# Product with `w_out` as seven half-size products, the `ple` product inside it, the gate product started tile by tile

## The chip, the core and the metric

The kernel runs on one core of one Trainium2 chip. The metric is the time of one execution in device microseconds (us); the median of three runs counts. The core has five instruction queues that run side by side and meet only through semaphores: PE (TensorE, matrix products and transposes), DVE (VectorE), ACT (ScalarE), POOL (GpSimd) and SP, which here only issues transfers.

## What is computed

A first block with attention and a short convolution, then a second block of two layers. Everything is float32, with 512 tokens of width 1024. The change lies at the end of the first block:

```python
mixed = jnp.concatenate([attn, conv_out], axis=-1) @ w_out[i]     # 512x1024 @ 1024x1024
x = x + rms_norm(mixed, post_norm_gain[i])                        # called x1 below

e = rms_norm(p[i] @ w_ple_proj[i], ple_norm_gain[i])              # 512x256 @ 256x1024
x = x + jax.nn.sigmoid(x @ w_ple_gate[i]) * e                     # 512x1024 @ 1024x1024
```

`attn` and `conv_out` are 512 columns wide each. Behind this comes the second block, whose first product (`v4`, with a 1024x2048 part of `a_w_in_2`) is already computed by seven half-size products for each half of its columns.

## The kernel before

**Split operands.** Each float32 operand of a large product is kept as a rounded part `hi` and a rest `lo`, and each product is three matmuls: hi·hi, hi·lo, lo·hi (`exact`, the lines 2076 to 2078). So each weight and each activation must be split before PE can use it. For the weights, a transfer of 512 KB brings half a unit into a room of `raw` or `gain`, one engine writes `whi` and one writes `wlo`. Units "by two" are split by ACT (`whi`, 1024 wide) and DVE (`wlo`, 1024 wide); all others by POOL alone (`whi` line 841, `wlo` line 850, 512 wide each). `whi` and `wlo` hold two units; a unit takes the slot of the unit two before it.

**Order.** `tensor_order` writes out by hand in what order PE works through its blocks, and `bank_of` says in which of eight PSUM banks a block's result lands. The other queues are written out by hand as well. Every queue is worked in order, so an instruction that waits holds up all that stand behind it on its engine.

**Around the change.** The last jobs of the projection stage are four heads of attention and the four feature tiles of the convolution. Their results go to `actB_hi`/`actB_lo`: attention in tiles 0 to 3 (DVE line 1609), convolution in tiles 4 to 7 (ACT line 1026, DVE line 1548). Then PE runs, in this order:

- `wo`: four units (two halves of the columns, two halves of the rows of `w_out`), each over four token tiles of 128: 192 matmuls of 512 columns. The results stay in the eight banks. In between, `p` is transposed.
- `ple`: 48 matmuls. Between its tiles, the pairs of transposes of x1 (line 2173).
- `gate`, first half of the columns: unit 0 (rows 0 to 511) over four token tiles, the transposes of the group weights (`wt`, line 2312), then unit 1, and so on.

x1 comes about like this: ACT squares the banks of `wo` with a sum (`square`, line 950); POOL makes the root (`root`, lines 795 and 798); DVE multiplies the bank by the root and the gain and adds the result to `resid` (`post`, lines 1618 and 1622, the wait being `x1_ready`); PE transposes `resid`; ACT writes `actA_hi` (`turned`, line 961) and DVE `actA_lo` (`rest`, line 1421, semaphore `lo_x1`). A gate block of token tile t waits for `lo_x1` of that tile.

**Seven products, as `v4` has them.** The activations are cut in two by tokens and in two by features, the weights in two by rows and columns. The seven products use sums of quarters. The four sums of activations are made one after the other: DVE `act_sum` (line 1679) writes a sum, ACT `sum_hi` (line 1122) its `hi`, DVE `act_sum_lo` (line 1683) its `lo`. The sums of weights are made by transfers that add to what lies in the room (`add_load`, issued by POOL). A product is 24 matmuls into two banks; `keep_v4` (line 1126) or `combine` (line 1696) takes it out, and `combine` adds it to parts of the result in `big`.

## Time and profile before

| | |
|---|---|
| median of three runs | 885.27 us (885.25 to 885.89) |
| the profiled execution | 885.75 us, span 884.0 us |
| PE busy | 868.2 us, 98% of the span |
| DVE, ACT, POOL busy | 537.2, 360.3, 542.8 us |
| granted TensorE clock | full in all 40 slices |
| bytes moved | 102.65 MB, mean 116 GB/s |

The span runs from the first to the last instruction; 1.75 us of the execution lie around it. "Busy" adds up the time in which an engine had work running. PE's rows overlap: a matmul of 512 columns is shown with 0.39 us, while the next starts 0.23 us after it. So the distance from one start to the next is the price of a matmul, and a wait shows as a larger distance between two starts.

### The profile page before, as it was taken

The page shows a single profiled execution, that of the slowest core. Times are in us where ns is not written, and L with a number is a line of the kernel's source. Part 1 is how long each engine was busy: PE and PEld are TensorE (multiplying, and loading weights), DVE is VectorE, ACT ScalarE, POOL GpSimd, SP SyncE. Part 2 cuts the span into 40 slices and gives each one's busy share as a digit, 9 for nine tenths or more (in the row PEclk, how much of TensorE's full clock was granted, in tenths as well). Part 3 has the DMA queues.
Part 4 walks back from the last instruction along what each step waited for, and adds up shares of the span by engine and source line. Part 5 has one row for each costly group of instructions (what it writes and reads, how often), then busy time and mean ns, then how long its engine had stood idle before and what let it go on. Part 6 is the DMA issues. An engine that isn't in the chain of part 4 may idle for free.

```text
span 884.0 us, 11936 instructions
## 1 busy us (share of the span) xinstructions
PE 868.2 (98%) x4220; PEld 722.0 (82%) x4220; DVE 537.2 (61%) x880; ACT 360.3 (41%) x804; POOL 542.8 (61%) x604
## 2 busy tenths in 40 slices
PE   8999999999999999999999999999997999999997
PEld 6888888888888787888888888888887888888886
DVE  6125648875035489775765535556996457788624
ACT  4123333431134377546112321113775536767622
POOL 7766556587789832317975038771359798566352
PEclk9999999999999999999999999999999999999999
DMA  7533231342322468885742253526962222112202
GB/s 198 167 120 96 74 92 51 96 143 92 128 90 96 124 146 177 208 203 190 162 124 95 73 190 96 125 90 152 217 180 71 72 73 93 51 49 72 73 1 95
DMA packets 81517, 102.65 MB, mean 116 GB/s; under 512 B 11826, under 2 KB 54322, under 8 KB 81459
## 3 DMA queue, kind: packets, MB, share of 16 engines
q1 hardware_dynamic: 72752, 85.12, 30.1%
q0 software_dynamic: 8704, 16.78, 11.2%
q8 instruction: 34, 0.56, 0.3%
q14 instruction: 25, 0.20, 0.1%
q10 hardware_dynamic: 2, 0.00, 0.0%
HBM read 99.79 MB, written 2.10 MB: 115 GB/s over the span
## 4 chain that ended last, share of the span: by engine, by line
PE 88%; POOL 4%; DVE 2%; DMA 2%; ACT 2%; issue 1%; POOLq 0%; DVEq 0%; ACTq 0%
PE bank L2076 26%; PE bank L2078 26%; PE bank L2077 26%; PE bank L2319 2%; PE bank L2347 1%; PE bank L2173 1%; DMA gain<-in_a_w_in 1%; DVE wlo L1667 1%; POOL wlo L850 1%; PE bank L2292 1%; PE bank L2342 1%; PE bank L2341 1%; DMA raw<-in_a_w_in 1%; POOL ms L795 1%; POOL whi L841 1%
## 5 line engine op out<-in xcount | busy, mean ns | idle before, releaser
L850 POOL TENSOR_TENSOR wlo<-raw,whi 128x512 fp32r<-128x512 f32 x204 | 280.4, 1404 | 0.7 <-ACT whi L972 0.7
L841 POOL TENSOR_SCALAR whi<-raw 128x512 fp32r<-128x512 f32 x202 | 140.8, 733 | 188.1 <-PE bank L2078 179.1
L2076 PE MATMUL bank<-actB_hi,whi 128*128 128x512 f32 (+1 forms) x416 | 159.6, 384 | 0.6 <-POOL wlo L850 0.6
L2077 PE MATMUL bank<-actB_lo,whi 128*128 128x512 f32 (+1 forms) x416 | 158.7, 381 | 0.0
L2078 PE MATMUL bank<-actB_hi,wlo 128*128 128x512 f32 (+1 forms) x416 | 158.5, 381 | 0.0
L2076 PE MATMUL bank<-whi,actA_hi 128*128 128x512 f32 x318 | 125.9, 396 | 1.2 <-DVE actA_lo L1421 0.7
L2078 PE MATMUL bank<-whi,actA_lo 128*128 128x512 f32 x318 | 124.0, 390 | 0.0
L2077 PE MATMUL bank<-wlo,actA_hi 128*128 128x512 f32 x318 | 123.9, 390 | 0.0
L2076 PEld LDWEIGHTS bank<-actB_hi,whi 128*128 128x128 f32 x416 | 78.3, 188 | 15.4 <-issue 1.1
L2078 PEld LDWEIGHTS bank<-actB_hi,wlo 128*128 128x128 f32 x416 | 78.2, 188 | 15.2
L2077 PEld LDWEIGHTS bank<-actB_lo,whi 128*128 128x128 f32 x416 | 78.3, 188 | 14.1
L2076 PE MATMUL bank<-actA_hi,whi 128*128 128x512 f32 x224 | 87.9, 392 | 0.0
L2077 PE MATMUL bank<-actA_lo,whi 128*128 128x512 f32 x224 | 87.4, 390 | 0.0
L2078 PE MATMUL bank<-actA_hi,wlo 128*128 128x512 f32 x224 | 87.3, 390 | 0.0
L2076 PEld LDWEIGHTS bank<-whi,actA_hi 128*128 128x128 f32 x318 | 59.7, 188 | 15.3 <-issue 1.9
L2078 PEld LDWEIGHTS bank<-whi,actA_lo 128*128 128x128 f32 x318 | 59.7, 188 | 12.6
L2077 PEld LDWEIGHTS bank<-wlo,actA_hi 128*128 128x128 f32 x318 | 59.8, 188 | 12.0 <-issue 0.2
L2076 PE MATMUL bank<-whi,actB_hi 128*128 128x512 f32 x144 | 56.5, 393 | 0.2 <-DVE wlo L1667 0.2
L2078 PE MATMUL bank<-whi,actB_lo 128*128 128x512 f32 x144 | 56.1, 390 | 0.0
L2077 PE MATMUL bank<-wlo,actB_hi 128*128 128x512 f32 x144 | 56.0, 389 | 0.0
L1776 DVE TENSOR_TENSOR acc<-acc,gcv 128x512 f32<-128x512 f32 x16 | 15.6, 974 | 58.3 <-ACT gcv L1228 58.3
L2078 PEld LDWEIGHTS bank<-actA_hi,wlo 128*128 128x128 f32 x224 | 42.1, 188 | 8.9
(269 smaller groups left out, 1579.4 us busy)
## 6 DMA issues: line engine op xcount, KB each, us to landing
raw<-in_a_w_in SPq DMA_DIRECT2D x44, 512.0 KB, 4.2
raw<-in_w_in SPq DMA_DIRECT2D x32, 512.0 KB, 3.9
raw<-in_b_w_in SPq DMA_DIRECT2D x16, 512.0 KB, 3.4
raw<-in_a_w_out SPq DMA_DIRECT2D x12, 512.0 KB, 3.3
gain<-in_a_w_out POOLq DMA_DIRECT2D x9, 512.0 KB, 8.2
raw<-in_w_out SPq DMA_DIRECT2D x8, 512.0 KB, 3.4
raw<-in_w_ple_gate SPq DMA_DIRECT2D x8, 512.0 KB, 3.3
gain<-in_a_w_in POOLq DMA_DIRECT2D x8, 512.0 KB, 7.7
```

The lines of the kernel that those rows point to most:

```text
L795: pool.tensor_scalar(m, ss[:, n, t, 0:1], ss[:, n, t, 1:2], EPS, ALU.add, ALU.add).then_inc(ms_ready, 1)
L841: pool.tensor_scalar(H, src[:, i * HALF:(i + 1) * HALF], 1.0, 1.0, ALU.mult, ALU.mult).then_inc(w_hi, 1)
L850: ins = pool.tensor_tensor(L, src[:, i * HALF:(i + 1) * HALF], H.bitcast(f32), ALU.subtract)
L1667: V.tensor_tensor(L, src, H.bitcast(f32), ALU.subtract).then_inc(w7_lo, 1)
L1776: V.tensor_tensor(acc[:, f % 2, :], acc[:, f % 2, :], gcv[:, f % 2, 0:S], ALU.mult).then_inc(zu_made, 1)
L2076: M(out_, whi_, xhi_, start=start, stop=False)
L2077: M(out_, whi_, xlo_, start=False, stop=False)
L2078: return M(out_, wlo_, xhi_, start=False, stop=stop)
L2173: ins = nc.tensor.transpose(bank[:, k * P:(k + 1) * P], src, ident[:, :])
L2292: ins = M(bank[:, qt * P:(qt + 1) * P], wgtT1[:, k * P:(k + 1) * P], tile(vtok, k)[:, h * P:(h + 1) * P], start=k == 0, stop=k == qt)
L2319: ins = M(bank[:, n * P:(n + 1) * P], big[:, n, f * P:(f + 1) * P], wcT[:, (f // 2) * P:(f // 2 + 1) * P], start=True, stop=True)
L2341: M(out_, q, khi(g)[:, keys], start=True, stop=False)
```

## The change

The four `wo` units become seven products `("S", "wo", q, r)`, q from 0 to 6, with two row tiles r. The quarters of `w_out` and their sums lie in rooms A, B and G; three of the sums are made by adding transfers. The result goes to `big` (`out_wo`) by the same `keep` and `combine` as in `v4`, and no longer stays in the banks. ACT and DVE split the weights of products 0, 1, 2, 3, 4 and 6 and of `ple`; POOL splits those of product 5. `ple` stands between products 4 and 5, with nothing in between its tiles. Its raw result goes to other parts of `big` (`e_raw`). The transposes of x1 stand behind product 6, each pair just ahead of the gate tile that reads it. `post` reads `out_wo` from `big` instead of a bank. The attention and convolution results also stay whole in `kT` and `zaT`, from which the sums of activations are made; for this the convolution's last multiplication writes to `zaT`.

```diff
-    u += [("wo", 2 * c + kh, "T", "w_out", 4 * kh, 512 * c) for c in range(2) for kh in range(2)]
+    u += [("wo", q, "S", "w_out", 0, 0) for q in range(5)]
     u += [("ple", 0, "P", "w_ple_proj", 0, 0)]
+    u += [("wo", q, "S", "w_out", 0, 0) for q in (5, 6)]
...
-    o += [("Th", "wo", 0, 0, t) for t in range(T)] + [("tr", "p", 0, k) for k in range(2)]
-    o += [("T", "wo", 0, 0, t) for t in range(T)]
-    o += [("T", "wo", 0, 1, t) for t in range(T)]
-    o += [("T", "wo", 1, kh, t) for kh in range(2) for t in range(T)]
-    for t in range(T):
-        o += [("ple", t, c) for c in range(2)]
-        if t:
-            o += [("tr", "x1", t - 1, j) for j in range(2)]
-    o += [("T", "gate", 0, 0, 0)] + [("tr", "x1", 3, j) for j in range(2)]
-    o += [("T", "gate", 0, 0, t) for t in range(1, T)] + [("wt", j) for j in range(2)]
+    o += [("S", "wo", q, r) for q in range(4) for r in range(2)] + [("tr", "p", 0, k) for k in range(2)]
+    o += [("S", "wo", 4, r) for r in range(2)] + [("ple", t, c) for t in range(T) for c in range(2)]
+    o += [("S", "wo", q, r) for q in (5, 6) for r in range(2)]
+    turn = lambda name, t: [("tr", name, t, j) for j in range(2)]
+    o += turn("x1", 0) + [("Th", "gate", 0, 0, 0)] + turn("x1", 1) + [("T", "gate", 0, 0, 0), ("T", "gate", 0, 0, 1)]
+    o += turn("x1", 2) + [("T", "gate", 0, 0, 2)] + turn("x1", 3) + [("T", "gate", 0, 0, 3)]
+    o += [("wt", j) for j in range(2)]
...
-            after[at("ple", 0, 0)] = [lambda: root("m1", 0, D)]
-            after[at("ple", 0, 1)] = [lambda t=t: root("m1", t, D) for t in range(1, T)]
+            after[at("wo", 5, 1)] = [lambda: root("m1", 0, D)]
+            after[at("gate", 0, 0) - 0.5] = [lambda: root("m1", 1, D)]
+            after[at("gate", 0, 0)] = [lambda: root("m1", 2, D)]
+            after[at("gate", 0, 1) - 0.5] = [lambda: root("m1", 3, D)]
...
+            after[at("b", 1, 1)] = [lambda: add_load("wo", 0, 3)]
+            after[at("zc", 1, 1)] += [lambda n=n: add_load("wo", 0, n) for n in (4, 6, 7)]
...
+            sum_hi(0, "wo")
+            hi_7("wo", 2)
+            for r in range(2):
+                keep_7("wo", 0, r)
+            sum_hi(1, "wo")
+            hi_7("wo", 3)
...
+            for t in range(2):
+                square_m1(2 + t, 1)
+            for t in range(2):
+                square_m1(t, 1)
+            for t in range(2):
+                square_m1(2 + t, 0)
+            for t in range(T):
+                for j in range(2):
+                    turned("x1", t, j)
...
-                    V.scalar_tensor_tensor(acc[:, c, :], psum[t + 4 * c][:, :], rstd[:, NORMS[name], t:t + 1],
+                    V.scalar_tensor_tensor(acc[:, c, :], out_wo(t, c), rstd[:, NORMS[name], t:t + 1],
```

**ACT, from the last convolution tile to `ple`.** Before, ACT copies the transposed `p` (line 959) and then only squares the banks of `wo`:

```order
L959 ACTIVATE actA_hi<-bank 128x512 [waits pe_block] x2
L950 ACTIVATE junk,ss<-bank 128x512 [waits attn_sq,pe_block]
L950 ACTIVATE junk,ss<-bank 128x512 [waits squared_m1,pe_block] x7
L1072 ACTIVATE big<-bank 128x512 [waits pe_block]
L950 ACTIVATE junk,ss<-bank 128x512 [waits squared_m1]
```

Now there stand here the `hi` parts of the sums of activations (line 1057) and of the weights of products 2 to 4 (line 1042), the copies of product 0 (line 1061) and two squares (line 982). The names `t_added` and `t3_added` are semaphores of the adding transfers:

```order
L1057 ACTIVATE actA_hi<-big 128x1024 [waits s7_made]
L1042 ACTIVATE whi<-raw 128x1024 [waits t_added0,pe_block]
L1042 ACTIVATE whi<-raw 128x1024 [waits t_added1]
L1061 ACTIVATE big<-bank 128x512 [waits pe_block] x2
L1057 ACTIVATE actA_hi<-big 128x1024 [waits s7_made]
L1042 ACTIVATE whi<-gain 128x1024 [waits t3_added0,pe_block]
L1042 ACTIVATE whi<-gain 128x1024 [waits t3_added1]
L1057 ACTIVATE actA_hi<-big 128x1024 [waits s7_made]
L982 ACTIVATE junk,ss<-big 128x512 [waits attn_sq,c7_made]
L982 ACTIVATE junk,ss<-big 128x512 [waits squared_m1,c7_made]
L1042 ACTIVATE whi<-raw 128x1024 [waits t_added0,pe_block]
```

Each `hi` of a sum now stands ahead of the two `hi` of the weights of the same product. In `v4` (before and now) both weight copies, or at least the first, stand ahead of the sum.

**DVE, where x1 is made.** Before, the four `post` stand one after the other, with the rests of one tile in between:

```order
L1618 SCALAR_TENSOR_TENSOR acc<-bank,rstd,gain 128x512 [waits rstd_m1,gain_in1]
L1618 SCALAR_TENSOR_TENSOR acc<-bank,rstd,gain 128x512
L1622 TENSOR_TENSOR resid<-resid,acc 128x1024 [waits post_scaled]
...
L1421 TENSOR_TENSOR actA_lo<-bank,actA_hi 128x4x128 [waits hi_x1] x2
```

Now the two combinations of product 6 (line 1686, waits `c7_made,pe_block`) stand between them, and the first operand of a `post` (line 1725) is `big`:

```order
L1725 SCALAR_TENSOR_TENSOR acc<-big,rstd,gain 128x512 [waits rstd_m1,gain_in1]
L1725 SCALAR_TENSOR_TENSOR acc<-big,rstd,gain 128x512
L1729 TENSOR_TENSOR resid<-resid,acc 128x1024 [waits post_scaled]
L1686 TENSOR_TENSOR big<-bank,big 128x512 [waits c7_made,pe_block]
L1725 SCALAR_TENSOR_TENSOR acc<-big,rstd,gain 128x512 [waits x1_ready,rstd_m1]
...
L1686 TENSOR_TENSOR big<-bank,big 128x512 [waits c7_made,pe_block]
L1476 TENSOR_TENSOR actA_lo<-bank,actA_hi 128x4x128 [waits hi_x1] x2
```

**PE, the transposes of x1.** Before, the twelve matmuls of a `ple` tile stand between two pairs of transposes (a pair is eight):

```order
L2173 MATMUL bank<-ident,resid 128x128 [waits x1_ready,squared_e]
L2173 MATMUL bank<-ident,resid 128x128 x3
...
L2076 MATMUL bank<-whi,actA_hi 128x512 [waits w_lo,lo_p,post_scaled]
L2077 MATMUL bank<-wlo,actA_hi 128x512
L2078 MATMUL bank<-whi,actA_lo 128x512
```

Now the matmuls of the gate follow directly on the transposes whose tile they read (`lo_x1`), tile 0 in two halves (`Th`, then `T`) with the transposes of tile 1 between them:

```order
L2268 MATMUL bank<-ident,resid 128x128 [waits x1_ready,c7_made]
L2268 MATMUL bank<-ident,resid 128x128 x3
...
L2171 MATMUL bank<-whi,actA_hi 128x512 [waits w_lo,lo_x1]
L2172 MATMUL bank<-wlo,actA_hi 128x512
L2173 MATMUL bank<-whi,actA_lo 128x512
```

## Rows read from the trace of the kernel before

**Rows 1.** The page's head and busy times (busy us, share of the span, instructions)

```profile
span 884.0 us, 11936 instructions
...
PE 868.2 (98%) x4220; PEld 722.0 (82%) x4220; DVE 537.2 (61%) x880; ACT 360.3 (41%) x804; POOL 542.8 (61%) x604
```

**Rows 2.** The chain of work that ended last, by engine

```profile
PE 88%; POOL 4%; DVE 2%; DMA 2%; ACT 2%; issue 1%; POOLq 0%; DVEq 0%; ACTq 0%
```

**Rows 3.** Busy time by engine: `wo`, then `ple` to the gate's unit 0

```profile
214.63:259.07 44.44, 44.44 (x201) 36.88 (x200) 9.52 (x10) 7.65 (x19) 33.58 (x36) 1.00 0.35 119
259.07:284.48 25.41, 25.41 (x130) 21.29 (x128) 15.53 (x19) 14.10 (x34) 24.64 (x26) 1.00 0.31 103
```

**Rows 4.** PE in order of time (start, us, what): the stage's edges

```profile
214.63 0.39 PE L2076 MATMUL bank<-whi,actB_hi 128*128 128x512 f32 x1
...
222.80 1.03 PE L2173 MATMUL bank<-ident,smC 128*128 128x128 f32 x8
...
259.07 0.39 PE L2076 MATMUL bank<-whi,actA_hi 128*128 128x512 f32 x1
...
284.48 1.04 PE L2312 MATMUL bank<-ident,gcv 128*128 128x128 f32 x8
```

**Rows 5.** DVE in order of time, around `wo` and where x1 is made

```profile
212.44 1.77 DVE L1609 TENSOR_TENSOR actB_lo<-big,actB_hi 128x512 fp32r<-128x512 f32 x1
...
216.19 1.79 DVE L1541 TENSOR_TENSOR acc<-acc,gcv 128x512 f32<-128x512 f32 x1
217.90 2.79 DVE L1548 TENSOR_TENSOR actB_lo<-acc,actB_hi 128x512 fp32r<-128x512 f32 x2
...
253.75 1.41 DVE L1618 SCALAR_TENSOR_TENSOR acc<-bank,rstd,gain 128x512 f32<-128x512 f32 x2 [28.40 <-POOL rstd L798]
255.19 1.61 DVE L1622 TENSOR_TENSOR resid<-resid,acc 128x1024 f32<-128x1024 f32 x1
...
276.66 1.29 DVE L1421 TENSOR_TENSOR actA_lo<-bank,actA_hi 128x512 fp32r<-128x512 f32 x2 [1.70 <-ACT actA_hi L961]
```

**Rows 6.** DVE in order of time inside `v4`

```profile
348.13 1.22 DVE L1679 TENSOR_TENSOR big<-big 128x1024 f32<-128x1024 f32 x1
349.26 1.22 DVE L1667 TENSOR_TENSOR wlo<-raw,whi 128x1024 fp32r<-128x1024 f32 x1
...
352.75 3.67 DVE L1696 TENSOR_TENSOR big<-bank,big 128x512 f32<-128x512 f32 x6
```

**Rows 7.** ACT in order of time: a square, a pair of x1, `v4` weights

```profile
261.13 0.59 ACT L950 ACTIVATE junk<-bank 128x512 f32<-128x512 f32 x1
261.60 0.20 ACT L950 ACTIVATION_READ_ACCUMULATOR junk<-bank 128x1 f32 x1
...
276.03 1.08 ACT L961 ACTIVATE actA_hi<-bank 128x512 fp32r<-128x512 f32 x2 [1.90 <-PE bank L2173]
...
347.17 1.99 ACT L1118 ACTIVATE whi<-raw 128x1024 fp32r<-128x1024 f32 x2
```

**Rows 8.** POOL in order of time: one root, one half unit of weights

```profile
258.05 0.30 POOL L795 TENSOR_SCALAR ms<-ss 128x1 f32<-128x1 f32 x1
258.44 0.58 POOL L798 TENSOR_TENSOR rstd<-ms,mhalf 128x1 f32<-128x1 f32 x1
...
272.58 1.20 POOL L841 TENSOR_SCALAR whi<-raw 128x512 fp32r<-128x512 f32 x2
273.76 2.53 POOL L850 TENSOR_TENSOR wlo<-raw,whi 128x512 fp32r<-128x512 f32 x2
```

**Rows 9.** Two DVE groups of one form, each over the whole program

```profile
L1903 DVE SCALAR_TENSOR_TENSOR resid<-big,rstd,resid 128x512 f32<-128x512 f32 x8 | 8.7, 1131 | 1.6 <-POOL rstd L798 1.6
...
L2065 DVE SCALAR_TENSOR_TENSOR resid<-big,rstd,resid 128x512 f32<-128x512 f32 x8 | 5.7, 749 | 1.4 <-POOL rstd L798 1.4
```

**Rows 10.** Transfers by line, KB each, median us to landing

```profile
raw<-in_a_w_in POOLq DMA_DIRECT2D x8, 512.0 KB, 7.6
```

**Rows 11.** PE in order of time, transposes near the program's start

```profile
7.94 1.92 PE L2173 MATMUL bank<-ident,tok 128*128 128x128 f32 x8
```

More of the change, by code:

```diff
@@ L66 @@
 WHOLE = {n: k for k, n in enumerate(n for n, u in enumerate(UNITS) if u[2] != "S")}
-BY_TWO = [n for n, u in enumerate(UNITS) if u[2] == "S" or u[:2] in (("z4", 0), ("z4", 4))]
+BY_TWO = [n for n, u in enumerate(UNITS) if u[2] == "S" and u[:2] != ("wo", 5)
+          or u[:2] in (("ple", 0), ("z4", 0), ("z4", 4))]
 TWO_NO = {n: k for k, n in enumerate(BY_TWO)}
@@ L105, in room_of @@
         return ROOM_A[j]
-    if s == "k5":
+    if s in ("k5", "ple"):
         return "K"
@@ L180 @@
 BANKS_F = ((1, 2, 0, 4), (5, 3, 6, 7))
-HEADS = {("v", 0, 0, t): 2 for t in range(T)} | {("wo", 0, 0, t): 3 for t in range(T)}
-HEADS |= {("gate", 1, 1, 3): 2}
+HEADS = {("v", 0, 0, t): 2 for t in range(T)}
+HEADS |= {("gate", 0, 0, 0): 2, ("gate", 1, 1, 3): 2}
 def tensor_order():
@@ new lines, in act_sum @@
+            def act_sum(i, s="v4"):
+                upper, lower = slice(0, S // 2), slice(S // 2, S)
+                one, two = feature(s, 0), feature(s, 1)
+                a11, a12, a21, a22 = one[:, :, upper], two[:, :, upper], one[:, :, lower], two[:, :, lower]
+                if i:
+                    dve.wait_ge(s7_lo, SUMS7[s] + i)
+                elif s == "v4":
+                    dve.wait_ge(h_copied, 2 * T)
+                else:
+                    dve.wait_ge(lo["attn"], NH1)
+                    dve.wait_ge(lo["conv"], 4)
+                place, first, second, op = ((a22, a21, a22, ALU.subtract), (a21, a11, a21, ALU.subtract),
+                                            (a22, a22, a11, ALU.subtract), (a22, a12, a22, ALU.add))[i]
+                V.tensor_tensor(place, first, second, op).then_inc(s7_made, 1)
@@ new lines, in act_sum_lo, with combine @@
+            def act_sum_lo(i, s="v4"):
+                dve.wait_ge(s7_hi, SUMS7[s] + i + 1)
+                V.tensor_tensor(s7(actA_lo, i), feature(s, 1 - (i == 1))[:, :, S // 2:S], s7(actA_hi, i).bitcast(f32),
+                                ALU.subtract).then_inc(s7_lo, 1)
+            def combine(g, m, place, other, op, waits, s="v4", rows=range(2)):
+                for r in rows:
+                    t, c = place
+                    u, d = other
+                    b = ("S", s, 7 * g + m, r)
+                    dve.wait_ge(pe_block, BLOCK[b])
+                    if waits:
+                        dve.wait_ge(c7_made, 14 * GROUP7[s, g] + waits + r)
+                    else:
+                        dve.wait_ge(x7_kept, 2 * GROUP7[s, g] + r + 1)
+                    V.tensor_tensor(out7(s, g, t + r, c), psum[bank_of(b)][:, :], out7(s, g, u + r, d), op)\
+                        .then_inc(c7_made, 1)
```

316 lines of the change are left out of this document (178 added, 138 removed).

## The prediction

> **What bounds the kernel now.** First the page's head and busy times [rows 1]: PE has work in 868.2 of 884.0 us, the next engine in 542.8. The chain that ended last says the same: 88% of it is PE [rows 2]. The table by stretches then narrows it down to the changed place [rows 3]: `wo` takes 44.44 us, `ple` with gate unit 0 25.41 us, and PE is busy in all of both. So two things count: how many matmuls go, and how long PE waits for operands that it does not wait for now. DVE is busy for 9.52 and 15.53 us there, ACT for 7.65 and 14.10. They have room on average; the question is whether they are in time.
>
> The price of a matmul follows from the two stretches. The first holds 192 matmuls and one group of eight transposes, the second 96 matmuls and four such groups. That gives 0.227 us for a matmul and 0.9 for a group. So a product of 24 costs 5.44 us, a gate tile of 12 costs 2.72, the half tile at its head 1.36. Nothing else in these stretches fits between: the edges lie at 214.63, 259.07 and 284.48 [rows 4].
>
> **What goes.** 192 matmuls become 168: 24 x 0.227 = 5.4 us less. That is all the change can give, 0.6% of the time.
>
> **Durations for what comes in.** DVE: a 1024-wide operation starts 1.13 us after the one before it, six combinations take 3.67, so 0.6 each [rows 6]. A free `post` is 1.2 for its two products and 1.15 for its sum, 2.4 together. ACT: two 1024-wide copies take 1.99 less the overlap, 0.95 each; a square with its sum 0.7 to 0.8; a pair of copies of x1 1.08, with DVE's first rest done 1.2 after the transposes [rows 5, 7]. POOL: a root 1.0, the `hi` of a half unit 1.2, its `lo` 2.5 [rows 8].
>
> **Front, products 0 to 4 and `ple`.** The clock of before is used. Product 0 needs the last attention rest, done at 212.44 + 1.77 = 214.2 [rows 5], and starts at 214.6 as now. It ends at 220.1. Product 1 needs the convolution's last rest. DVE now puts the two weight rests of product 1 (2.3 us) ahead of it. The slow 1.79 and 2.79 us [rows 5] become short again, as POOL no longer splits weights here: 216.2 + 0.6 + 0.6 + 2.3 + 0.6 = 220.4. Wait 0.3. Then begins the loop over the sums of activations: sum (DVE 1.13), its `hi` (ACT 0.95), first half of the weights' `hi` (ACT 0.95), weight rest, rest of the sum, second weight rest (DVE 3 x 1.13), 0.2 for hand-overs, together 6.6. A product lasts 5.44. In `v4` this loop is closed by DVE alone, 4 x 1.13 = 4.6, as ACT has a weight copy ready early [rows 6]; here ACT makes the sum's `hi` first and DVE stands idle for two copies. Product 2 is just met (+0.2), product 3 comes 1.2 late (232.5 for 231.3), product 4 is 0.8 late behind the transposes of `p`, because two squares (1.5) stand ahead of its weights. `ple` follows the same two queues: sum 3, its `hi` and rest, two copies and two rests of its own weights, `p` copied and split last. This is done at 247.5, while product 4 ends at 245.1: 2.5 late. Front: 0.3 + 0.2 + 1.2 + 0.8 + 2.5 = **5.0 us**. Products 5 and 6 have `ple` (10.9 us) as cover for their weights. If ACT had the weights early, the front would wait 1 us at least (the convolution and `p`).
>
> **Tail, x1 and the gate.** Set 0 at the end of product 6. Before, `ple` covered this chain. Now only product 6 (5.44) covers tile 0, and nothing covers the rest. Tile 0 is ready at about 0: the squares of product 5 end at -4.7, root -3.7, `post` 2.4 to 3.7. Its transposes end at 0.9. But ACT's copies of tile 0 stand behind the squares of product 6, and the last of those waits for a combination that stands behind `post` of tile 1 on DVE.
>
> - All free: 0.6 (combination) + 2.4 (`post` 1) + 0.6 (combination) + 0.8 (square) + 0.6 (copy) + 0.6 (rest) = 5.6, so PE waits 4.7. The second half of gate unit 0 is split behind roots 2 and 3: 1.2 more. Tile 1 is in time. Tiles 2 and 3 each wait for their own copy and rest, 1.2 each. Sum 8.3.
> - With POOL in the way: `post` now reads `big` and `gain`, both in SBUF, while POOL splits gate weights beside it. Before it read a bank, and took 1.41 for two with POOL busy; its SBUF-only sum took 1.61 for 1.15 [rows 5]. The attention rest took 1.77 and the convolution product 1.79 where 0.68 is free. So each of the three operations may lose up to a whole POOL operation (1.05 to 1.25), and `post` becomes 5.2 on the mean. Then tile 0: 0.6 + 5.2 + 0.6 + 0.8 + 0.6 + 0.6 = 8.4, wait 7.5. POOL, delayed the same way, has the second half of unit 0 at 12.0, for 10.7: 1.3. DVE then makes rests to 9.0, `post` 2 to 14.2, rest of tile 1 at 14.9, for 13.4: 1.5. `post` 3 ends at 20.7, rest of tile 2 at 21.4, for 18.5: 2.9. Tile 3 waits 1.2 for copy and rest. Sum **14.4**.
>
> I take the second, because the rows with POOL's split directly beside show nearly a full operation lost. The mean of a whole group says less: one form takes 1131 ns where POOL is at work and 749 where it is not [rows 9], 0.4 for an operation; with that `post` is 3.6 and the tail about 11, which lies between the bounds.
>
> The Trainium skill ("SBUF — State Buffer", section "SBUF: two separate sides") says that a VectorE instruction with two SBUF inputs and a GpSimd instruction share a port pair as an exclusive lock, held for the whole instruction. By that rule every operation of `post` may wait for a whole `lo` of POOL (1.27), and the sum would be +15; by the mean of the group it would be +11.
>
> Later stages: PE stays the bound, and nothing there waits long enough to give the time back.
>
> **Sum.** -5.4 + 5.0 + 14.4 = +14.0. The profiled execution has 884.0 in the span and 1.75 around it; the change gives 898.0 + 1.75 = 899.8. The median lies 0.5 below that execution, so **899.3 us**. The ends: front 1 and tail 8.3 give +3.9, front 5 and tail 8.3 +7.9, front 5.5 and tail 16 +16.
>
> **Rivals.**
> - *The port costs little.* Speaks for it: POOL also has roots and waits in between, and the group mean in rows 9. Then front 5.0, tail 8.3: 893.2.
> - *The clock falls in the long wait.* PE stands still for 7.5 us. Near the start eight transposes took 1.92 us [rows 11] where later 1.03 is usual [rows 4], half speed. Tile 0 at half speed costs 2.7 + 0.9 more, of which the waits for weights and tile 1 take up 1.3 + 1.5 again: 900 to 903. Against it: nothing in before stands still so long, so no row tests it.
> - *An adding transfer is late.* They land 7.6 us after issue [rows 10]. The one for product 2 is issued at about 208 and needed at 222; those for product 4 at about 227 and 237; each has some 2 to 6 us to spare. Late by as much again, 904.
> - *Faster.* ACT and DVE run ahead as in `v4` (front 0), and tile 0 is all that waits, 4.7: -5.4 + 4.7 = 884.6. This decides as soon as all waits together fall below 5.4. Against it: in the front the order of ACT's queue alone gives 1.2 a product, and in the tail `post` 1 stands ahead of the last square in any case.
>
> In a sentence apart: the Trainium skill ("TensorE: Matmul & The Clock Gate", section "Part 1: The HAM clock gate") says that an idle TensorE is put back to 1.2 GHz; by that rule the second rival holds, and the time is up to 903.
>
> **Chances.** Forecast (waits 17 to 22, 896 to 902) 0.57; port cheap (891 to 896) 0.16; clock 0.13; late transfer 0.05; faster 0.05; no change 0.04. The likeliest gives 899.3. The range must leave out 0.2: 892 to 904 leaves out the last two and the far parts of the second and the fourth. What lies within 0.2% (1.8 us) of before can hardly be told from no change. Faster by more 0.05, within 0.04, slower 0.91.
>
> **What the trace after would show.** Each product has 24 matmuls at 0.227. PE has a gap of about 1 us ahead of product 3 and product 4, 2 to 3 ahead of `ple`, none ahead of 5 and 6. Behind the transposes of tile 0 there is the largest gap, 7 to 8 us (5 if the port is free), released by DVE's rest. `post` operations take 1.3 to 1.9 instead of 0.7. The gate's four tiles have gaps before each, falling to 1.2 at tile 3. `wo` to the group transposes takes 69.9 - 5.4 + 19.4 = 83.9 us. Wrong would be: ACT's copies of tile 0 directly behind their transposes, a `post` of 2.4 throughout, or a granted clock below full.

## The result and the profile after

| | before | after |
|---|---|---|
| median | 885.58 us (885.25 to 887.77, 4 runs) | 901.13 us (898.81 to 901.77, 4 runs) |
| profiled execution, its span | 885.75, 884.0 us | 900.76, 898.6 us |

The ratio is 1.0165 with a 95% interval of 1.0141 to 1.019: slower by 15 us. (The median of before is 0.3 above that of the first table, since a fourth run has come in.) Each experiment below is compared with a median of before taken on the same chip; these lie between 885.3 and 886.5.

The page's head, busy times and granted clock in 40 slices, after; [rows 1] shows head and busy times before, where the clock was full in all 40 slices:

```profile
span 898.6 us, 11933 instructions
PE 868.5 (97%) x4196; PEld 719.7 (80%) x4196; DVE 572.0 (64%) x916; ACT 378.8 (42%) x824; POOL 522.5 (58%) x580
PEclk9999999999998999999999999999999999999999
```

PE is busy as long as before with 24 matmuls fewer, and one slice has a clock below full. So something went slower, and something waited. The table by stretches, to be held beside [rows 3]; the stretches are products 0 to 4; `ple` with products 5 and 6; and from the transposes of tile 0 to the group transposes. Columns: stretch and its length, busy time (count) of PE, PE's weight loads, DVE, ACT, POOL, then granted clock, DMA share, GB/s:

```profile
214.30:247.72 33.42, 29.39 (x129) 22.99 (x128) 25.99 (x27) 18.63 (x25) 6.95 (x7) 1.00 0.73 176
247.72:271.21 23.49, 23.49 (x97) 19.18 (x98) 11.94 (x16) 14.07 (x34) 10.37 (x12) 0.93 0.28 92
271.21:298.60 27.39, 17.28 (x81) 13.82 (x80) 22.31 (x21) 5.78 (x12) 26.30 (x28) 0.88 0.24 77
```

There are three kinds of stretch. The first loses time to waits at full clock. The second has PE busy throughout, and loses to the clock alone (0.93 of full on the mean). The third has PE busy for 17.3 of 27.4 us, while DVE and POOL are busy for nearly all of it.

PE's timeline gives every edge (start, duration, line; in brackets the idle time and who ended it), as [rows 4] does for before:

```profile
214.33 0.39 PE L2171 MATMUL bank<-whi,actB_hi 128*128 128x512 f32 x1
220.16 0.47 PE L2171 MATMUL bank<-whi,actB_hi 128*128 128x512 f32 x1 [0.22 <-issue]
232.63 0.47 PE L2171 MATMUL bank<-whi,actA_hi 128*128 128x512 f32 x1 [0.99 <-DVE actA_lo L1672]
239.68 0.47 PE L2171 MATMUL bank<-whi,actA_hi 128*128 128x512 f32 x1 [0.44 <-DVE wlo L1644]
247.72 0.47 PE L2171 MATMUL bank<-whi,actA_hi 128*128 128x512 f32 x1 [2.32 <-DVE actA_lo L1473]
271.21 1.03 PE L2268 MATMUL bank<-ident,resid 128*128 128x128 f32 x8
278.70 0.77 PE L2171 MATMUL bank<-whi,actA_hi 128*128 128x512 f32 x1 [6.46 <-DVE actA_lo L1476]
281.39 1.70 PE L2268 MATMUL bank<-ident,resid 128*128 128x128 f32 x8
284.88 0.47 PE L2171 MATMUL bank<-whi,actA_hi 128*128 128x512 f32 x1 [0.40 <-DVE actA_lo L1476]
287.73 1.04 PE L2268 MATMUL bank<-ident,resid 128*128 128x128 f32 x8
290.99 0.47 PE L2171 MATMUL bank<-whi,actA_hi 128*128 128x512 f32 x1 [2.23 <-DVE actA_lo L1476]
293.83 1.03 PE L2268 MATMUL bank<-ident,resid 128*128 128x128 f32 x8
295.88 0.47 PE L2171 MATMUL bank<-whi,actA_hi 128*128 128x512 f32 x1 [1.02 <-DVE actA_lo L1476]
298.71 1.03 PE L2408 MATMUL bank<-ident,gcv 128*128 128x128 f32 x8
```

From these rows the loss is worked out. The whole takes 84.4 us; before it took 69.9. Each piece between two rows holds a known number of matmuls (0.227) and transpose groups (0.9); what is left over is loss. Products 0 to 4 lose 0.4 + 1.6 + 0.7 + 2.6 = **5.3**. From 247.72 to 271.21 stand 96 matmuls (21.8), in 23.5: **1.7**. Behind the transposes of tile 0 comes a wait of **6.6**. The half tile behind it, six matmuls, takes 2.7 where 1.4 is due, and the next transposes 1.46 for 0.9: **1.9** together. Then 0.7 ahead of tile 1, 2.4 ahead of tile 2, 1.2 ahead of tile 3 and 0.2 in between: **4.5**. The sum is 20.0, less 5.4 for the 24 matmuls: +14.5. The spans differ by 14.6, and 0.4 more lies around the span (2.16 for 1.75).

What stands behind the two pieces lost in "busy" time is shown by the granted clock:

```profile
244.00:250.00 6.00, 3.68 (x14) 2.70 (x13) 6.00 (x10) 1.79 (x4) 4.42 (x5) 0.88 0.70 126
250.00:256.00 6.00, 6.00 (x23) 4.80 (x23) 2.40 (x5) 4.41 (x11) 3.64 (x4) 0.83 0.44 149
276.00:280.00 4.00, 1.30 (x3) 1.14 (x4) 2.73 (x5) 1.69 (x4) 3.82 (x7) 0.50 0.26 100
280.00:284.00 4.00, 4.00 (x17) 3.33 (x17) 3.97 (x3) 1.20 (x2) 4.00 (x3) 0.66 0.31 96
```

Both times PE had just stood still, for 2.3 and 6.5 us. Behind the longer wait its matmuls start 0.43 us apart at once, the lower level of 1.2 GHz. Behind the shorter one the first matmuls still start 0.23 to 0.32 apart, and the lower level holds from 248.8 to 251.8.

The tail on DVE, to be held beside [rows 5]: `post`'s two products (L1725) and its sum (L1729), and the rests that PE waits for (L1476):

```profile
271.40 3.37 DVE L1725 SCALAR_TENSOR_TENSOR acc<-big,rstd,gain 128x512 f32<-128x512 f32 x2
274.81 1.23 DVE L1729 TENSOR_TENSOR resid<-resid,acc 128x1024 f32<-128x1024 f32 x1
...
277.90 1.29 DVE L1476 TENSOR_TENSOR actA_lo<-bank,actA_hi 128x512 fp32r<-128x512 f32 x2 [1.27 <-ACT actA_hi L993]
279.11 3.03 DVE L1725 SCALAR_TENSOR_TENSOR acc<-big,rstd,gain 128x512 f32<-128x512 f32 x2
282.17 2.00 DVE L1729 TENSOR_TENSOR resid<-resid,acc 128x1024 f32<-128x1024 f32 x1
285.30 3.44 DVE L1725 SCALAR_TENSOR_TENSOR acc<-big,rstd,gain 128x512 f32<-128x512 f32 x2
288.77 1.52 DVE L1729 TENSOR_TENSOR resid<-resid,acc 128x1024 f32<-128x1024 f32 x1
```

And on ACT, the last square of product 6 and, only behind it, the copies of tile 0, whose transposes had been ready since 272.1:

```profile
276.67 0.63 ACT L982 ACTIVATE junk<-big 128x512 f32<-128x512 f32 x1 [4.42 <-DVE big L1686]
...
277.30 1.06 ACT L993 ACTIVATE actA_hi<-bank 128x512 fp32r<-128x512 f32 x2
```

`post` 1 to 3 take 4.5 to 5.0 us each, from the first product to DVE's next operation; `post` 0, beside less work of POOL, takes 3.2.

### The profile page after: what moved, and what is told of

The parts are those of the page before. It is cut to its first block, busy times and chain, and to the rows that moved or that the text cites. A ratio compares the mean times of both kernels' runs of the same rounds, so it can differ in the third digit from the quotient of the medians.

```text
span 898.6 us, 11933 instructions
## 1 busy us (share of the span) xinstructions
PE 868.5 (97%) x4196; PEld 719.7 (80%) x4196; DVE 572.0 (64%) x916; ACT 378.8 (42%) x824; POOL 522.5 (58%) x580
## 4 chain that ended last, share of the span: by engine, by line
PE 82%; DVE 7%; POOL 4%; ACT 3%; issue 2%; DMA 1%; DVEq 0%; POOLq 0%; SPq 0%; ACTq 0%
PE bank L2171 25%; PE bank L2173 24%; PE bank L2172 24%; DVE wlo L1644 2%; PE bank L2415 2%; POOL wlo L878 1%; PE bank L2443 1%; DVE acc L1725 1%; PE bank L2388 1%; PE bank L2438 1%; DMA raw<-in_a_w_in 1%; PE bank L2437 1%; DVE big L1668 1%; PE bank L2268 1%; POOL rstd L822 1%
## 5 line engine op out<-in xcount | busy, mean ns | idle before, releaser
L878 POOL TENSOR_TENSOR wlo<-raw,whi 128x512 fp32r<-128x512 f32 x188 | 256.6, 1395 | 0.8 <-ACT whi L1004 0.8
L869 POOL TENSOR_SCALAR whi<-raw 128x512 fp32r<-128x512 f32 x186 | 133.8, 757 | 179.4 <-PE bank L2173 173.9
L2171 PE MATMUL bank<-whi,actA_hi 128*128 128x512 f32 x350 | 139.8, 400 | 15.8 <-DVE actA_lo L1476 10.8
L2173 PE MATMUL bank<-whi,actA_lo 128*128 128x512 f32 x350 | 137.5, 393 | 0.0
L2172 PE MATMUL bank<-wlo,actA_hi 128*128 128x512 f32 x350 | 137.5, 393 | 0.0
L2173 PEld LDWEIGHTS bank<-whi,actA_lo 128*128 128x128 f32 x350 | 66.4, 190 | 14.3
L2172 PEld LDWEIGHTS bank<-wlo,actA_hi 128*128 128x128 f32 x350 | 66.4, 190 | 13.4 <-issue 0.2
L1644 DVE TENSOR_TENSOR wlo<-raw,whi 128x1024 fp32r<-128x1024 f32 x28 | 33.4, 1221 | 29.2 <-ACT whi L1042 29.2
L2172 PEld LDWEIGHTS bank<-actA_lo,whi 128*128 128x128 f32 x224 | 42.1, 188 | 8.3
L2171 PEld LDWEIGHTS bank<-actA_hi,whi 128*128 128x128 f32 x224 | 42.1, 188 | 8.3
```

Source lines behind the costliest of these rows:

```text
L869: pool.tensor_scalar(H, src[:, i * HALF:(i + 1) * HALF], 1.0, 1.0, ALU.mult, ALU.mult).then_inc(w_hi, 1)
L878: ins = pool.tensor_tensor(L, src[:, i * HALF:(i + 1) * HALF], H.bitcast(f32), ALU.subtract)
L1644: V.tensor_tensor(L, src, H.bitcast(f32), ALU.subtract).then_inc(w7_lo, 1)
L2171: M(out_, whi_, xhi_, start=start, stop=False)
L2172: M(out_, whi_, xlo_, start=False, stop=False)
L2173: return M(out_, wlo_, xhi_, start=False, stop=stop)
```

## The experiments

All are edits of the changed kernel; from the one with `ple` last on, they build on one another. Times after a label are medians.

### The order of ACT's queue in the front

```diff
-            sum_hi(0, "wo")
             hi_7("wo", 2)
+            sum_hi(0, "wo")
...
-            sum_hi(1, "wo")
             hi_7("wo", 3)
+            sum_hi(1, "wo")
...
             for k in range(2):
                 turned("p", 0, k)
+            sum_hi(3, "wo")
```

`hi_7("wo", 4)` goes ahead of the sum in the same way; on DVE the rest of sum 3 goes behind those of `ple`'s weights and of `p`.

> Only the order of ACT's and DVE's queues in the front changes: both halves of a product's weights are copied before the copy of the sum, and `p` before the last sum. Theory (ACT's order makes the front late): the waits of 1.15 us before product 3 and 2.5 us before `ple` go, and with the second of them the half-speed stretch behind it (1.75 us lost), so 901.1 - 1.1 - 2.4 - 1.7 = 896 us (895 to 897.5), PE gaps in the front below 0.5 us each. Rival (DVE is the late one, the order on ACT is not): the gaps stay and so does the time, 900 to 902. Rival (the clock is not tied to the wait): 897.5 to 898.5, gap gone but the half-speed matmuls remain.

Measured: 895.75 us (895.15 to 896.24), ratio 1.0114 (1.0099 to 1.013). The two stretches up to `ple` and into it:

```profile
214.00:244.00 30.00, 29.77 (x135) 24.16 (x134) 25.45 (x26) 18.75 (x25) 5.25 (x5) 1.00 0.72 180
244.00:256.00 12.00, 12.00 (x55) 9.90 (x54) 5.20 (x9) 9.63 (x25) 7.68 (x8) 1.00 0.57 141
```

PE is busy for 41.8 of the 42 us, at full clock; in the changed kernel it was busy for 38.0 of the same 42 us, with the clock at 0.86 in the last 12. So it was the order of the queues, and in the front the half-speed stretch is gone with the wait. The theory holds, with its number. For the waits between the products only ACT's order was changed; for the one ahead of `ple` DVE's rest of sum 3 was moved too, so its 2.5 us belong to both queues together. The tail's first wait is as it was, 6.45 us. In this execution the clock also fell behind the wait ahead of tile 2 (2.0 us), where it had stayed full in the changed kernel; the tail took 29.1 us for 27.5.

### `post` with a bank as input

```diff
-                    V.scalar_tensor_tensor(acc[:, c, :], out_wo(t, c), rstd[:, NORMS[name], t:t + 1],
+                    V.scalar_tensor_tensor(acc[:, c, :], psum[3][:, :], rstd[:, NORMS[name], t:t + 1],
```

> The two products of `post` read a PSUM bank in place of `big`, so that they have one SBUF tensor as input and not two; the values that they then work on are not the product's, so x1 and what follows from it are left wrong in content, the work is the same. Theory (POOL and `post` stand in each other's way at the SBUF port): the two products fall from 3.0 to 3.4 us to about 1.4 for two, `post` from 4.5 to 5.0 to 2.6 to 3.5, the wait after tile 0's transposes from 6.6 to about 4.5, the one before tile 2 goes; 901.1 - 4.5 = 896.6 us (895.5 to 898.5). Rival (the operations are long for another reason, or something else is late): under 1 us, 900 to 902.

Measured: 896.92 us (896.64 to 898.33), ratio 1.0131 (1.0117 to 1.0145). DVE's `post` 1, and PE's waits ahead of tiles 0 and 2:

```profile
269.41 1.40 DVE L1725 SCALAR_TENSOR_TENSOR acc<-bank,rstd,gain 128x512 f32<-128x512 f32 x2
270.85 2.04 DVE L1729 TENSOR_TENSOR resid<-resid,acc 128x1024 f32<-128x1024 f32 x1
275.55 0.77 PE L2171 MATMUL bank<-whi,actA_hi 128*128 128x512 f32 x1 [4.67 <-DVE actA_lo L1476]
286.74 0.47 PE L2171 MATMUL bank<-whi,actA_hi 128*128 128x512 f32 x1 [1.02 <-DVE actA_lo L1476]
```

The products take 1.4 for two beside the same work of POOL; the sum, still with two SBUF inputs, takes 2.0 to 2.3. The waits fall from 6.5 to 4.7 and from 2.2 to 1.0. So the second SBUF input was what made them long. The median falls by 4.2 us. Of the 4.1 us between the two profiled executions only 2.9 lie in the tail (from the transposes of tile 0 to the group transposes, 24.6 us for 27.5); 1.6 lie in the front, which is the same code, where this time the clock did not fall behind the wait of 2.4 us; elsewhere 0.4 is lost. So the crowded products cost 3 to 4 us here. The Trainium skill ("SBUF — State Buffer", section "SBUF: two separate sides") tells it so, an exclusive lock between a VectorE operation with two SBUF inputs and GpSimd; by these rows the trace agrees, for `scalar_tensor_tensor` too.

### Both at once

The edits of the two kernels above.

> Both edits of e1_act and e2_bank in one kernel; as in e2_bank `post` works on values of a bank that are not the product's, so x1 and what follows are left wrong in content. Theory (front and tail are separate sums): 901.1 - 5.4 - 4.2 = 891.5 us (890.5 to 893), which leaves 5.9 us over before, made of -5.4, 0.6 in front and the rest in the tail (free-port sum of 8.3 and what the clock takes). Rival (they share a loss, the half-speed stretch ahead of `ple` or one that only moves): 893 to 896.

Measured: 891.52 us (890.71 to 892.13), ratio 1.007 (1.0056 to 1.0083). The medians add up: 901.13 - 5.4 - 4.2 = 891.5. With the front repaired in both, the products' second SBUF input is worth 4.2 again by the medians (895.75 to 891.52), and in the profiled executions 4.8 in the tail (29.1 to 24.3 us). This includes the half speed behind the wait ahead of tile 2, which is gone as that wait shrinks from 2.0 to 1.0. What is left over before, 6.2 us, is in the main the tail without the crowded products.

### Tile 0's copies first

```diff
+            for j in range(2):
+                turned("x1", 0, j)
             for t in range(2):
                 square_m1(2 + t, 0)
-            for t in range(T):
+            for t in range(1, T):
```

On DVE both combinations of product 6 and tile 0's rests go ahead of `post` 1.

> In the tail alone: ACT copies tile 0's transposes ahead of product 6's last squares, DVE makes both combinations of product 6 and tile 0's rests ahead of `post` 1. Theory (what is late is the whole chain of four `post` operations of 4.5 to 5 us on DVE, not the place of one copy in a queue): the wait ahead of the gate's first matmul shrinks from 6.6 to about 3, but `post` 1 now starts 2 us later and tiles 1 to 3 and the roots 2 and 3 with it, so the wait comes back ahead of tile 1 and of the second half of tile 0; the time stays at 899.5 to 902. Rival (the order of the queues is the tail's bound): the 3.5 us stay gone, 897 to 898.5.

Measured: 901.47 us (901.22 to 901.74), ratio 1.0183 (1.0169 to 1.0197). PE's waits in the tail:

```profile
274.04 0.47 PE L2173 MATMUL bank<-whi,actA_hi 128*128 128x512 f32 x1 [1.70 <-POOL wlo L878]
276.60 1.06 PE L2270 MATMUL bank<-ident,resid 128*128 128x128 f32 x8 [0.93 <-DVE resid L1731]
283.20 0.77 PE L2173 MATMUL bank<-whi,actA_hi 128*128 128x512 f32 x1 [5.54 <-POOL wlo L878]
```

The head of the gate starts 4.7 us earlier, and the largest wait now stands one block on. The time is the same, as expected, but the cause that I named holds only in part: PE waits longest for POOL's second half of the weights, not for DVE. POOL's `hi` of that half took 2.35 us where 1.20 is usual, and a root 2.0, while `post` ran beside it. So POOL loses time beside `post` as well, and with no cover the tail has two chains of nearly the same length, DVE's x1 and POOL's weights. Making one of them earlier gives nothing by itself.

### PE kept at work in the wait

```diff
-    o += turn("x1", 0) + [("Th", "gate", 0, 0, 0)] + ...
+    o += turn("x1", 0) + [("fill", 0), ("Th", "gate", 0, 0, 0)] + ...
...
+                if kind == "fill":
+                    for n in range(12):
+                        ins = M(bank[:, :], actB_hi[:, 0, 0:P], actB_lo[:, 0, :], start=True, stop=True)
+                    return ins
```

The first kernel holds 12 added matmuls, the second one 24.

> 24 added... see the count in the code: 12 matmuls of 512 columns with nothing to do with the result run in the long wait behind tile 0's transposes (2.7 us of its 6.6), into a free bank. Theory (the clock falls in that wait because PE stands still, and costs about 1.8 us until the weights' and tile 1's waits take part of it back): if 2.7 us of work are enough to keep it, the gate's first matmuls come 0.227 apart and the time is 901.1 - 1 to 1.8 = 899.3 to 900.1; if the fall only moves to later, they stay 0.43 apart and the time is 901. Rival (the fall has nothing to do with the wait): no change, 900.5 to 901.5.

> As e4_warm (which held 12), with 24 added matmuls that have nothing to do with the result: 5.4 us of the 6.6 us behind tile 0's transposes. Theory (the clock falls because PE stands still there, and 12 were too few): gate tile 0 runs at 0.227 a matmul, 1.2 us earlier done, of which the wait for tile 1 takes part: 899.5 to 900.5, unless the clock falls in the next wait ahead of tile 2 instead, then 900.5 to 901.5. Rival (the fall does not hang on the wait): the head's matmuls stay 0.43 apart.

Measured: 900.73 us (898.8 to 901.25) with 12, 900.75 us (900.3 to 902.24) with 24; neither can be told from 901.13. With 12 the head still runs at half speed (matmuls 0.43 apart from 277.65), and it does so again in tile 2. With 24 the wait ahead of the head shrinks to 1.0 and the clock is full there. It falls later instead, behind the wait of 2.25 us ahead of tile 2. The transposes of tile 0, the first matmul of tile 1, and the stretch in which it fell:

```profile
271.63 1.03 PE L2268 MATMUL bank<-ident,resid 128*128 128x128 f32 x8
285.36 0.47 PE L2171 MATMUL bank<-whi,actA_hi 128*128 128x512 f32 x1 [1.52 <-DVE actA_lo L1476]
292.00:296.00 4.00, 4.00 (x12) 3.01 (x11) 0.00 (x0) 0.00 (x0) 3.54 (x7) 0.57 0.26 84
```

So the fall of the clock hangs on PE standing still, but filling one gap of several gives nothing back. The rows say why: tile 1 starts 13.7 us behind the transposes of tile 0 with the head at full speed (271.63 to 285.36) and at half speed (271.21 to 284.88 in the changed kernel), because PE waits there for DVE in any case. Half speed in the head only fills a wait. This also fits the other executions: three of the five with 24 were granted 0.998 of full clock on the mean, more than any after the change (0.993 to 0.995), and still took 900.3 to 901.3. (With 12, the clock in the front stayed full in the profiled execution, 1.00 from 244 to 256, behind the same wait of 2.4 us. It stayed full there in the kernel with a bank as input too. So a wait of this length is followed by a fall in some executions and not in others.)

### `ple` back behind the products

```diff
-    u += [("wo", q, "S", "w_out", 0, 0) for q in range(5)]
+    u += [("wo", q, "S", "w_out", 0, 0) for q in range(7)]
     u += [("ple", 0, "P", "w_ple_proj", 0, 0)]
-    u += [("wo", q, "S", "w_out", 0, 0) for q in (5, 6)]
...
+    o += [("S", "wo", q, r) for q in (4, 5, 6) for r in range(2)]
+    o += [("ple", t, c) for t in range(2) for c in range(2)] + turn("x1", 0)
+    o += [("ple", 2, c) for c in range(2)] + turn("x1", 1) + [("ple", 3, c) for c in range(2)]
+    o += [("Th", "gate", 0, 0, 0), ("T", "gate", 0, 0, 0)] + turn("x1", 2) + [("T", "gate", 0, 0, 1)]
+    o += turn("x1", 3) + [("T", "gate", 0, 0, 2), ("T", "gate", 0, 0, 3)]
```

> The seven products stay, `ple` stands behind the seventh with the x1 transposes of tiles 0 and 1 inside it, those of 2 and 3 behind the first two gate tiles; ACT and DVE split all of `w_out`'s weights and `ple`'s, POOL only the gate's; the front has e1_act's order. Theory (the tail is dear because nothing covers x1, and all the rest is hidden again by 10.9 us of `ple`): no wait above 1 us between the products and the group transposes, 885.6 - 5.4 + 0.5 to 3 = 881 to 884 us. Rival (port: `post` of 4.5 to 5.0 is too long even for this cover, tiles 2 and 3 are 3 to 6 us late): 885 to 889. Rival (seven products with their sums cost the front more than the 5.4 us that they save, wherever `ple` stands): 886 to 890 with the waits before products.

Measured: 889.12 us (887.63 to 889.5), ratio 1.0035 (1.0022 to 1.0047). The tail of 6.6 and more is gone, but my number was missed by 5 us: this is at the upper edge of the rivals, and by neither's cause alone. Four waits are new, two of them ahead of product 6 and of `ple`, and two for POOL's split of the gate's weights:

```profile
251.93 0.50 PE L2173 MATMUL bank<-whi,actB_hi 128*128 128x512 f32 x1 [1.67 <-DVE wlo L1647]
257.54 0.47 PE L2173 MATMUL bank<-whi,actA_hi 128*128 128x512 f32 x1 [1.24 <-DVE wlo L1654]
274.09 0.47 PE L2173 MATMUL bank<-whi,actA_hi 128*128 128x512 f32 x1 [1.82 <-POOL wlo L878]
301.47 0.47 PE L2173 MATMUL bank<-whi,actA_hi 128*128 128x512 f32 x1 [1.37 <-POOL wlo L878]
```

Ahead of product 6, ACT's copy of the weights had itself waited for a transfer:

```profile
249.56 1.06 ACT L1040 ACTIVATE whi<-raw 128x1024 fp32r<-128x1024 f32 x1 [5.01 <-DMA raw<-in_w_out]
```

It was issued by POOL at 237.6, some 12 us earlier. With `ple` between products 4 and 5 there was time for it. The next kernel moves only two gain rows and `b_s` (three loads of 512 KB) to behind gate unit 1. This moves two more: `ple`'s weights stand behind `b_s` in SP's queue and were issued at 238.4, right beside the adding transfer; now they go at 232.0.

> e3_pleL with one thing changed: two gain rows and `b_s` are loaded behind the gate's second unit and not beside the adding transfer for product 6. Theory (that transfer was late because it shared the DMA engines: 11 us from issue to use where 7.4 is the median): ACT no longer waits for DMA there, the wait of 1.7 us ahead of product 6 goes, the one ahead of `ple` stays or grows by a part of it: 887.2 to 888.5 where e3_pleL had 889.1. Rival (DVE's six combinations are what is late ahead of product 6): 889 to 889.5.

Measured: 887.59 us (886.69 to 888.35), ratio 1.0022 (1.0013 to 1.0032): 1.5 us less by the medians, 1.2 by the ratios, whose intervals overlap. What the profile shows is firmer: the wait ahead of product 6 is gone, and ACT has both halves in time:

```profile
243.36 2.01 ACT L1042 ACTIVATE whi<-raw 128x1024 fp32r<-128x1024 f32 x2 [2.43 <-PE bank L2177]
```

### The remaining waits, one after the other

The next kernel adds to this buffers of its own for gate unit 0, and other places for the roots and the group transposes.

```diff
-SLOTTED = [n for n, u in enumerate(UNITS) if u[0] != "v5"]
+SLOTTED = [n for n, u in enumerate(UNITS) if u[0] != "v5" and u[:2] != ("gate", 0)]
...
-            if UNITS[n][0] == "v5":
+            if UNITS[n][0] == "v5" or UNITS[n][:2] == ("gate", 0):
                 return v5hi[:, w], v5lo[:, w]
...
+            after[at("gate", 0, 1)] = [lambda t=t: root("m1", t, D) for t in range(T)]
```

> e3_pleL with its four waits addressed: two gain rows and `b_s` are loaded later, so that they don't stand beside the adding transfer for product 6; ACT copies `ple`'s weights ahead of two squares; gate unit 0 gets buffers of its own (v5hi, v5lo, not in use then), so POOL splits it and gate unit 1 early, all four roots ahead of unit 1; `e`'s roots come after gate unit 2, the group transposes `wt`, `rw` in gate unit 2. Theory (only waits stand between the seven products and their 5.4 us): left are some 0.6 in the front, 1 to 3 around tiles 2 and 3, where `post` is still crowded, up to 2.8 ahead of `rw`; 885.6 - 5.4 + 0.6 + 3.5 = 884.3 us (882 to 886.5). Rival (the port's loss only moves, since POOL now works beside DVE's weight rests too): 887 to 890, waits before products 5, 6 or `ple`.

Measured: 887.68 us (885.31 to 889.26, 10 runs), ratio 1.0025 (1.0015 to 1.0034). Missed again, and no less than the kernel before it. What is left is one wait and the clock behind it. DVE's rows of `post` 0, while POOL makes roots, and of `post` 3, while POOL splits gate unit 1; then the rests of tile 2 behind it, and PE at gate tile 2:

```profile
258.50 1.41 DVE L1729 SCALAR_TENSOR_TENSOR acc<-big,rstd,gain 128x512 f32<-128x512 f32 x2 [2.37 <-POOL rstd L822]
259.94 1.22 DVE L1733 TENSOR_TENSOR resid<-resid,acc 128x1024 f32<-128x1024 f32 x1
271.15 3.45 DVE L1729 SCALAR_TENSOR_TENSOR acc<-big,rstd,gain 128x512 f32<-128x512 f32 x2
274.64 1.51 DVE L1733 TENSOR_TENSOR resid<-resid,acc 128x1024 f32<-128x1024 f32 x1
276.86 0.77 PE L2174 MATMUL bank<-v5hi,actA_hi 128*128 128x512 f32 x1 [2.83 <-DVE actA_lo L1480]
```

This is the cost of the two SBUF inputs seen without any change of data: the same operations take 1.41 and 1.22 beside roots of one column, 3.45 and 1.51 beside POOL's rests of 512 columns. Behind the wait of 2.8 us, eleven distances between matmuls are 0.42 or 0.43, 2.3 us lost. So the next kernel makes tile 2's rests ahead of `post` 3; on PE, tile 0 of gate unit 1 goes ahead of tile 3's transposes:

```diff
-                if 1 <= t < 3:
+                for u in {1: (0,), 2: (1, 2), 3: (3,)}.get(t, ()):
                     for j in range(2):
-                        rest("x1", t - 1, j)
+                        rest("x1", u, j)
```

> e7_best with one thing changed: DVE makes tile 2's rests ahead of `post` 3 (5.0 us with POOL beside it) and not behind it, and gate unit 1's tile 0 stands ahead of tile 3's transposes. Theory (the one wait of 3.0 us ahead of gate tile 2, and the half-speed stretch behind it, are all that kept e7_best above before): both go, 887.7 - 2.8 - 2.6 = 882.3 us (881.5 to 884), granted clock at 1.00 between 270 and 300. Rival (the wait moves on, to the tile 3 rests, to gate unit 2's weights or to `rw`, since DVE and POOL have the same work in less time): 884 to 887, and the clock falls there.

Measured: 884.92 us (883.54 to 887.49, 11 runs), ratio 0.9994 (0.9986 to 1.0003). The wait in the tail is gone, and the clock is full from 270 to 300; 2.8 of the expected 5.4 us came. In the profiled execution there is another wait, 1.94 us ahead of `ple`, with the clock at 0.72 in the 6 us behind it. The edit did not bring it: up to that place the code is that of the kernel before, which waits 0.32 there. And with `e`'s roots in the middle of gate unit 2:

```diff
-            after[at("gate", 2, 1)] = [lambda t=t: root("e", t, D) for t in range(T)] + [mask_ws]
+            after[at("gate", 2, 1)] = [mask_ws]
+            after[at("gate", 2, 0)] = [lambda t=t: root("e", t, D) for t in range(2, T)]
+            after[at("gate", 1, 1)] = [lambda t=t: root("e", t, D) for t in range(2)]
```

> e9_rest with `e`'s roots 0 and 1 ahead of gate unit 2 on POOL and 2 and 3 in the middle of it, not all behind it. Theory (POOL has some 8 us to spare there): as e9_rest within 1 us, 882 to 884; if e9_rest waits at `rw` for ACT, this one doesn't. Rival (POOL is too full): gate unit 2's weights are late by 2 to 4 us, 885 to 888.

Measured: 883.27 us (882.54 to 886.09, 11 runs), ratio 0.9977 (0.9969 to 0.9986). This is 0.2% faster than before. How much of the 1.65 us to the kernel above is the edit's is open: in its profiled execution the wait ahead of `ple` was 0.32 us, and that place is not what was edited. From `ple` to the gate no wait of PE above 0.4 us is left, and the clock is full; the stretch in which the first of these kernels waited for tile 2:

```profile
274.00:280.00 6.00, 6.00 (x28) 4.84 (x27) 2.65 (x3) 0.00 (x0) 5.63 (x9) 1.00 0.28 90
```

But one further on has grown: PE reaches `v4` earlier and waits there for 2.35 us at product 4, for a sum whose copy on ACT stands behind a late adding transfer. The last kernel puts the copy of the sum between the halves of the weights:

```diff
+                if q == 3:
+                    hi_v4(4, (0,))
+                    sum_hi(2)
+                    hi_v4(4, (1,))
-                if 1 < q < 13:
+                elif 1 < q < 13:
                     hi_v4(q + 1)
```

> e11_roots with one thing changed, in the stage behind the gate: ACT copies the sum of activations for `v4`'s product 4 between the two halves of the weights for `v4`'s product 4, not behind both. Theory (the 2.4 us that PE waits there come from the second half's adding transfer, which lands late however early PE gets there, and the sum's copy only stands behind it): the wait falls by the 1.4 us that two of four k-steps of half a product cover, 883.3 - 1 to 1.5 = 882 us (881.3 to 882.8). Rival (the same time is lost at the second half of the weights): 883 to 883.5.

Measured: 881.77 us (881.48 to 884.15, 5 runs) against 886.49 for before in the same set, ratio 0.995 (0.9936 to 0.9964). The wait at `v4`'s product 4 is gone. This is the best version: the seven products with `ple` behind them, 0.5% faster than before. (Against the kernel above that is 1.5 us by the medians and 2.4 by the ratios, since before was 1 us slower in this set.) Its profiled execution is the slowest of the five, and shows where the wait ahead of `ple` comes from. DVE's rests of `ple`'s weights, 1.21 each in the kernel before it, take nearly twice as long beside POOL's:

```profile
249.65 2.22 DVE L1661 TENSOR_TENSOR wlo<-tok,whi 128x1024 fp32r<-128x1024 f32 x1
252.99 2.27 DVE L1661 TENSOR_TENSOR wlo<-tok,whi 128x1024 fp32r<-128x1024 f32 x1
255.92 0.50 PE L2177 MATMUL bank<-whi,actA_hi 128*128 128x512 f32 x1 [1.97 <-DVE big L1696]
```

Here POOL began to split gate unit 0 at 245.0, as soon as its weights had landed, and so it did at 245.2 in the profiled execution of the kernel with tile 2's rests ahead of `post` 3, which has the same wait. In the profiled executions just before those two in the series, with a wait of 0.32, it began at 246.8 and 247.2, and the rests took 1.21. The code is the same in all four up to there, so the wait comes in some executions and not in others.

## Why the prediction was right, and where not

The prediction was 899.3 us with a range of 892 to 904; 901.1 was measured. The mechanism was right: two sums of waits, in the front by the order of the queues, in the tail by a chain of DVE operations without cover. Its likeliest case (waits of 17 to 22 us in all) came about in the sum, 20.0 for 19.4 us. That it came so near is in part luck: the front lost 7.0 for 5.0, the tail 13.0 for 14.4, and the two misses nearly cancelled. One of the signs of being wrong that the prediction names did show, a granted clock below full. Term by term:

- **24 matmuls fewer, -5.4.** Right: each product has 24 starts 0.227 apart.
- **Front, 5.0.** Measured 5.3: 0.4, 0.3, 1.3, 0.7, 2.6 ahead of products 1 to 4 and `ple`, forecast 0.3, 0.2, 1.2, 0.8, 2.5. The cause was named rightly, as the first experiment shows: ACT copies the sum ahead of the weights (ahead of `ple` together with DVE's order).
- **The clock in the front.** Not forecast. The rival put the fall only behind the long wait of the tail; it fell behind 2.3 us too, and took 1.7. This is the step that was incomplete: "Front: 5.0" was made up of waits alone.
- **Tile 0, 7.5.** Measured 6.6. `post` 1 took 4.55, not 5.2: its sum lost nothing (1.23; POOL's root beside it took 1.43 where 0.57 is usual), its products did (3.37 for 1.4). The chain (`post` 1, combination, square, copy, rest) stands in the rows as the prediction has it.
- **The second half of the weights, 1.3, and tile 1, 1.5.** Measured 0 and 0.7. The half-speed head and transposes (1.9) took their place, as the rival on the clock said. With 24 added matmuls and the head at full speed these waits are there (0.7 and 1.7), and tile 1 starts no earlier. So this fall of the clock cost next to nothing.
- **Tiles 2 and 3, 2.9 and 1.2.** Measured 2.4 and 1.2; `post` 3 took 5.0.
- **The stretch, 83.9.** Measured 84.4, with the clock in it.
- **The port.** I took the full loss of an operation for `post`. Shown in two ways: with a bank as input of the products, the sums still crowded, the tail falls by 2.9 to 4.8 us and the median by 4.2 (14.4 - 8.3 = 6.1 forecast for all three operations), and in the version with `ple` last the same `post` is short or long depending on what POOL does. The loss is most of a POOL operation for a product (1.0 each), and between nothing and 0.8 for the sum. A whole POOL operation lost by each of the three was right as a bound and too dear as a price.
- **"An adding transfer is late"** did not happen here: none of PE's waits goes back to one. It happened as soon as `ple` no longer stood in front of the last products.
- **"Nothing there waits long enough to give the time back"** held for this change (1.2 us ahead of `v4`'s product 4, for 0.4 before), but not in the other direction: 2 us that the better version had gained were lost again in `v4` until its queue was changed.

That the cover was what the tail lacked is shown as well. With `ple` behind the products, the tail's waits of 11 us are down to waits that have other causes, and with those addressed the version is 2.2 us faster than before (883.27 for 885.51), and 4.7 with the edit in `v4`. That edit is no part of the seven products; it was not run on the kernel of before, which I expect to win little by it, since its own wait there is 0.4 us (starts at 345.33 and 345.98 for 0.23 apart).

Not settled: why a wait of 2.3 us brings the clock down in some executions and not in others. The fall was seen behind waits of 1.9 to 6.5 us, but behind those of 1.7 and 1.8 us ahead of product 6 and the gate in the first kernel with `ple` last it did not come. It also did not come behind 2.2 us ahead of tile 2 in the changed kernel. What decides it was not tried.

## What to carry to other kernels

A smaller product saves its matmuls once, but its operands have chains of their own; where several engines make them, count each queue in its order, and put what the other engine waits for ahead of what it has early. Moving a cover (here `ple`) is dearer than the saving if a chain of DVE operations lies bare behind it; look first for what can stand in front of it. A VectorE operation that loses its PSUM input costs nothing in its own row of a quiet trace (1.41 us for two products either way), and up to 2.4 times its time beside GpSimd's operations of 512 columns (3.45). Look at the granted clock behind each new wait, and remove the wait: filling one of several gaps with matmuls of no use gave nothing back. Half speed costs time only where the next tile's operands are ready.
